# Moving a prologue's adaptive vectors from VectorE to single-column matmuls on TensorE

## The chip, the cores and the metric

The kernel runs on one core of a Trainium2 chip. A core has TensorE (PE, matmuls, with PEld for its weight loads), VectorE (DVE), ScalarE (ACT), GpSimd (POOL) and SyncE (SP), which here issues the weight transfers. The metric is the device time of one execution in microseconds (us). Three runs of the kernel before took 2280.79, 2285.01 and 2287.35 us, median 2285.01.

## The reference

Two transformer-like blocks run one after the other over the same activations x (256 tokens, 1024 features), two layers each, in float32. This case touches only the first half of each layer of the first block:

```
ada = silu(c) @ w_ada[l] + b_ada[l]                 # c: one vector of 1024; w_ada: 1024 x 6144
sh_m, sc_m, g_m, sh_f, sc_f, g_f = split(ada, 6)    # six vectors of 1024
h = rms_norm(x, norm_mix[l]) * (1 + sc_m) + sh_m
q_a, kc_a, vc_a, ks_a, ..., q_b, k_b, v_b, g_br = split(h @ w_in[l])
y_a = nsa_mixer(...)     # compressed keys and values: gelu(blocks @ w1) @ w2; selected; window
y_b = moba_mixer(...)
```

The first norm needs sh_m and sc_m of layer 0, that is the first 2048 of the 6144 columns of `silu(c) @ w_ada[0]`. Nothing of the projections can start before it.

## The kernel before

Each engine has its own program in one file, written out by hand, and they meet only at semaphores (`sig` and `at`). Nothing is scheduled by a planner.

**Panels.** All weights stream through `ring`, three slots of 1 MB (128 partitions x 2048 floats), in the order of the list that `weight_panels` makes. SyncE waits until the panel three places earlier is `released` and issues the next. A "split" panel is cut in a high and a low part for exact float32 products: ScalarE copies the high part to `parts` (L647), VectorE subtracts to get the low part (L2009, "parts<-ring,parts"), which also releases the slot. `parts` has two slots, so ScalarE first waits until TensorE has used the panel two places earlier. TensorE then does three products per weight and chunk (L1329). "raw" panels (the first weights of the compression, `cw1`) are read from the ring by TensorE itself (L1560), and TensorE's last matmul on one releases it.

**Prologue.** The adaptive columns come in groups of 512, each in two panels of 4 x 128 rows. In layer 0 the groups 0 to 3 lead the list. VectorE multiplies every 128 x 512 piece by one element per partition of silu(c) and adds it up in `sq` (L2013, L2018), and TensorE sums the 128 partitions by four matmuls with a column of ones (`ada_cols`, L1340). A float32 matmul of this kind is two passes, hence x8 in the profile. After all four groups the norm starts: one chunk of 128 features after the other is scaled and shifted on VectorE, its high part goes through ScalarE, its low part back through VectorE. The rotation angles (`angles`, then Sin on ScalarE) come after the norm.

**Projections.** `first_block` runs the column groups of w_in in the order 1, 0, 2, 3 (`ORDER`): group 1 holds the compression's inputs; `blocks` on VectorE lays them out after four transposes per kind ("tr blk"), eight additions "feat<-psum,pe_t". The eight steps of group 2 are interleaved with the 32 matmuls of the compression's hidden layer (`hidden_steps`), keys and values both. ScalarE applies gelu to them, then Sigmoid to the gates, then goes on to group 3's panels. TensorE turns q and the selected keys while group 3 runs.

**Attention.** A loop over 24 heads follows (`head_steps`, LAG 2): per turn TensorE makes one head's scores, turns the probabilities of the head two earlier, weights the values of the one before that, and takes two steps of later projections (`beside`, 12 matmuls of 512 columns per turn at first, PSUM banks 2 and 3). The compressed branch is threaded through at given turns. PSUM banks are taken by `open_bank`, which waits until the last holder of the bank is freed.

The steps of the prediction touch the first projections in both layers (0 and 1) of the first block, since `first_block(l)` runs for both, and the prologue, which is there once.

## Time and profile before

| | |
|---|---|
| median of three runs | 2285.01 us |
| the profiled execution | 2285.55 us, of which the span of its instructions 2283.7 us |
| PE / PEld busy | 2086.5 us (91%) / 1965.8 us (86%) |
| DVE / ACT / POOL busy | 1471.2 us (64%) / 993.5 us (44%) / 27.5 us (1%) |
| DMA | 372.84 MB, mean 163 GB/s |
| mean granted TensorE clock | 0.945 of full |

"Busy" is an average over stages with different limits. The prologue is a small part of the span and is limited by other things than the rest.
### The profile page before, as it was taken

How to read it: one execution, taken by the hardware profiler on the slowest of the kernel's cores; microseconds unless marked ns; L12 is line 12 of the kernel's file. 1: busy time of each engine (PE TensorE's matmuls, PEld its weight loads, DVE VectorE, ACT ScalarE, POOL GpSimd, SP SyncE). 2: the span in 40 equal slices, each digit the busy share in tenths (PEclk: the TensorE clock that was granted, in tenths of full speed). 3: DMA queues.
4: the chain of work that ended last, by engine and by line, in shares of the span. 5: the costliest groups of instructions: out<-in, count | busy, mean ns of one | idle time of the engine just before them, and what ended most of it. 6: DMA issues, size and time to landing. Idle time of an engine off the chain costs nothing. (4 is left out here: it accounts for less than half of the span.)

```text
span 2283.7 us, 36579 instructions
## 1 busy us (share of the span) xinstructions
PE 2086.5 (91%) x15232; PEld 1965.8 (86%) x15232; DVE 1471.2 (64%) x2521; ACT 993.5 (44%) x1502; POOL 27.5 (1%) x47
## 2 busy tenths in 40 slices
PE   3799979997799889999999988899999997788999
PEld 2668879997679879999998777799999996678999
DVE  6568667876577566547756576577567657555773
ACT  2355534333445433334335554543343445554342
POOL 0101000000001000000000000000000000000000
PEclk7899999999889999999999998999999998799999
DMA  8335547883544347555555323355555553232554
GB/s 285 127 133 197 182 129 247 260 278 121 167 147 168 122 137 228 181 183 183 182 175 190 119 74 111 111 167 185 179 174 183 175 163 107 74 102 83 185 180 134
DMA packets 266086, 372.84 MB, mean 163 GB/s; under 512 B 8385, under 2 KB 160193, under 8 KB 265921
## 3 DMA queue, kind: packets, MB, share of 16 engines
q1 hardware_dynamic: 264224, 367.48, 49.3%
q8 instruction: 121, 1.98, 0.4%
q10 hardware_dynamic: 1696, 3.02, 0.4%
q14 instruction: 45, 0.36, 0.0%
HBM read 369.41 MB, written 1.05 MB: 162 GB/s over the span
## 5 line engine op out<-in xcount | busy, mean ns | idle before, releaser
L2009 DVE TENSOR_TENSOR parts<-ring,parts 128x2048 fp32r<-128x2048 f32 (+4 forms) x307 | 677.7, 2209 | 471.1 <-ACT parts L647 470.7
L1329 PE MATMUL psum<-h,parts 128*128 128x256 f32 x7656 | 937.7, 284 | 27.2 <-DVE parts L2009 20.8
L1329 PEld LDWEIGHTS psum<-h,parts 128*128 128x128 f32 x7656 | 926.9, 193 | 30.2 <-issue 29.7
L647 ACT ACTIVATE parts<-ring 128x2048 fp32r<-128x2048 f32 (+3 forms) x308 | 569.5, 1849 | 863.6 <-PE psum L1329 781.7
L1329 PE MATMUL psum<-hid_hl,parts 128*128 128x256 f32 x3168 | 378.9, 282 | 1.1 <-DVE parts L2009 1.1
L1329 PEld LDWEIGHTS psum<-hid_hl,parts 128*128 128x128 f32 x3168 | 377.0, 188 | 2.0 <-issue 1.9
L1329 PE MATMUL psum<-parts,h 128*128 128x512 f32 (+1 forms) x960 | 256.3, 426 | 49.1 <-DVE parts L2009 49.1
L1329 PEld LDWEIGHTS psum<-parts,h 128*128 128x128 f32 x960 | 196.3, 214 | 93.7 <-issue 28.6
L2228 DVE CUSTOM_DVE_ANT_0 scores_area<-psum,const 128x128 f32<-128x128 f32 (+1 forms) x144 | 45.5, 353 | 102.6 <-PE psum L1497 102.6
L1497 PE MATMUL psum<-feat 64*128 64x128 f32 (+4 forms) x320 | 81.1, 380 | 15.4 <-ACT feat L647 10.0
L647 ACT ACTIVATE scores_area<-scores_area,nmax 128x256 f32<-128x256 f32 (+1 forms) x160 | 72.0, 453 | 45.9 <-DVE nmax L2228 45.4
L2009 DVE TENSOR_TENSOR rot<-psum,rstd 128x256 f32<-128x256 f32 x176 | 66.5, 419 | 38.7 <-PE psum L1329 33.4
L647 ACT ACTIVATE scores_area<-psum 128x384 f32<-128x384 f32 (+1 forms) x80 | 39.6, 498 | 107.5 <-PE psum L1509 107.4
L1497 PEld LDWEIGHTS psum<-feat 64*128 64x128 f32 (+2 forms) x320 | 48.1, 205 | 30.2 <-ACT feat L647 11.9
L2009 DVE TENSOR_TENSOR hid_hl<-rot,hid_hl 128x256 fp32r<-128x256 f32 x132 | 56.1, 425 | 4.5
L1329 PE MATMUL psum<-y_ab,parts 128*128 128x256 f32 x384 | 51.1, 298 | 7.4 <-DVE parts L2009 3.6
L1329 PE MATMUL psum<-y_mix,parts 128*128 128x256 f32 x384 | 51.5, 296 | 6.6 <-DVE y_mix L2009 3.4
L1329 PEld LDWEIGHTS psum<-y_ab,parts 128*128 128x128 f32 x384 | 50.2, 205 | 8.2 <-DVE parts L2009 3.8
L1522 PE MATMUL psum<-tok,scores_area 128*128 128x64 f32 (+1 forms) x368 | 51.3, 279 | 6.1 <-ACT scores_area L647 4.2
L1329 PEld LDWEIGHTS psum<-y_mix,parts 128*128 128x128 f32 x384 | 49.5, 201 | 7.2 <-DVE y_mix L2009 3.8
L2018 DVE SCALAR_TENSOR_TENSOR feat<-ring,scol,feat 128x512 f32<-128x512 f32 x70 | 53.3, 762 | 3.2
L2018 DVE SCALAR_TENSOR_TENSOR tok<-ring,scol,tok 128x512 f32<-128x512 f32 x70 | 52.6, 752 | 3.2
(224 smaller groups left out, 1669.1 us busy)
## 6 DMA issues: line engine op xcount, KB each, us to landing
ring<-in_w_ada SPq DMA_DIRECT2D x48, 1024.0 KB, 5.4
ring<-in_w_ffn_in SPq DMA_DIRECT2D x88, 512.0 KB, 5.0
ring<-in_ffn_w_gate SPq DMA_DIRECT2D x88, 512.0 KB, 4.0
ring<-in_ffn_w_up SPq DMA_DIRECT2D x88, 512.0 KB, 5.0
ring<-in_w_in SPq DMA_DIRECT2D x36, 1024.0 KB, 5.1
ring<-in_ffn_w_down SPq DMA_DIRECT2D x32, 1024.0 KB, 5.0
ring<-in_w_ffn_out SPq DMA_DIRECT2D x16, 1024.0 KB, 5.0
ring<-in_ffn_w_down SPq DMA_DIRECT2D x16, 768.0 KB, 4.4
```

Of the source, the lines that this page charges most:

```text
L647: act.activation(out, in_, func, **kw).then_inc(*sig(name, *keys))
L1329: mm = pe.matmul(out, left, right, start=start and n == 0, stop=stop and n == 2, skip_group_check=True)
L1497: mm = pe.matmul(b[:, a:c], head["q"][:, P * t:P * t + P], head["k"][:, 0:c - a], start=True, stop=True)
L1522: mm = pe.matmul(head["o"][t], prob_t[:, (base + i) % 2, o:o + P], head["v"][n], start=n == 0, stop=o == c - P)
L2009: dve.tensor_tensor(out, a, b, op).then_inc(*sig(name, *keys))
L2018: dve.scalar_tensor_tensor(out=out, in0=a, scalar=s, in1=b, op0=op0, op1=op1, **kw).then_inc(*sig(name, *keys))
L2228: dve.tensor_tensor_reduce(to, of, add, -scale, 3.0e38, ALU.add, ALU.min, nmax[:, n % 3, t:t + 1]).then_inc(*sig("dve_nmax", *keys))
```

## The change

- The panels of the adaptive groups come in the order 2, 3, 0, 1 (the scale vector first, then the shift), the last group behind the panels of w_in's group 1.
- VectorE's products go. TensorE reads the raw panels from the ring: 16 matmuls per panel (4 row chunks x 4 column blocks), weights 128 x 128 from the panel, one moving column of silu(c) (`first_ada`). Its last matmul releases the panel. The matmuls of the norm's statistics stand behind the first group, group 1 behind three of the eight steps of w_in's first group. The norm takes its vectors in two portions (`vectors`).
- `angles` and the Sin run ahead of everything.
- Of the constants the first 416 columns are loaded at the start; the other 1416, the rows of gains (864 KB), `pe_t` and `w2` are issued by SyncE after the eleventh panel.
- The raw panels of the compression are spread through the panel list. Its hidden layer is split: keys beside group 2, values beside group 3. Gelu and the gates' Sigmoid on ScalarE stand behind group 3's evacuation. The compressed branch comes some turns later in the attention loop. VectorE splits both panels of group 0 before the heads and blocks of group 1.

```diff
-ADA_FIRST = 4
+ADA_FIRST = (2, 3, 0, 1)
...
-CONSTS = (("ident", 128), ("ones", 128), ("tri", 128), ("causal", 384), ("chunked", 384),
...
+CONSTS = (("ident", 128), ("ones", 128), ("tri", 128), ("inv", 32), ("causal", 384),
...
+N_FIRST = 416
...
+    for i in ADA_FIRST:
+        for n in range(2):
+            src = rows(w["w_ada"][0])[:, 4 * n:4 * n + 4, 512 * i:512 * i + 512]
+            out.append((("ada", 0, i, n), "first", [(0, src)]))
+    late = out[6:]
+    del out[6:]
     for l in range(L):
         win = w["w_in"][l]
         for i in ORDER:
             group(("win", l), i, win, EDGES[i], EDGES[i + 1])
...
+            out += late
+            late = []
+            if i >= 2:
+
+                kv, name = i - 2, ("nsa_cmp_k_w1", "nsa_cmp_v_w1")[i - 2]
+                for n in range(2):
+                    src = rows(w[name][l])[:, CMP // 2 * n:CMP // 2 * n + CMP // 2, :]
+                    out.insert(len(out) - 1 + n, ((("cw1", l), kv, n), "raw", [(0, src)]))
...
+                if n == 10:
+
+                    for name, dst, src in (
+                            ("masks", const[:, N_FIRST:N_CONST], w["const"][:, N_FIRST:N_CONST]),
+                            ("rows", rowsb[:], w["rows"].broadcast_to([P, N_ROW])),
+                            ("pe", pe_t[:], w["pe_t"]), ("w2", w2[:], w["w2"])):
+                        sp.dma_start(dst, src).then_inc(
...
+            def first_ada(i):
+
+                key = ("ada", 0, i)
+                b = open_bank(key, (BANKS + i,))
+                for half in range(2):
+                    v = raw((*key, half), 4, 512)
+                    pe.wait_ge(*at(("panel", (*key, half))))
+                    for c in range(4):
+                        for j in range(4):
+                            mm = pe.matmul(b[:, j:j + 1], v[:, c, P * j:P * j + P],
+                                           scol[:, 4 * half + c:4 * half + c + 1],
+                                           start=half + c + j == 0, stop=half == 1 and c == 3,
+                                           skip_group_check=True)
...
                 if l == 0:
+                    pe.wait_ge(*at("silu c"))
+                    first_ada(ADA_FIRST[0])
                     stats(st, squares, 4)
                     stats(st, squares, DC, 4, psum[:, tally.banks[("stats", st)], :])
-                    for i in range(ADA_FIRST):
-                        ada_cols(0, i, (BANKS + i,))
+                    for i in ADA_FIRST[1:3]:
+                        first_ada(i)
...
-                whole_of(win(1))
+                steps = win(1)
+                if l == 0:
+                    advance(steps, 3)
+                    first_ada(ADA_FIRST[3])
+                whole_of(steps)
...
                 for i in ORDER:
-                    splits.until((("win", l), i, 1), 1 if i == 1 else 2)
+                    splits.until((("win", l), i, 1), 2)
```

How the instructions stand on TensorE at the start of the program, before: eight matmuls with the squares of x, then four groups of four, each waiting for VectorE's sum, then the projections.

```order
L1317 MATMUL psum<-tok,const 128x256 [waits act_squares,dve_step,load_const]
L1317 MATMUL psum<-tok,const 128x256 [waits act_squares] x7
L1340 MATMUL psum<-const,sq 128x1 [waits dve_ada]
L1340 MATMUL psum<-const,sq 128x1 x3
L1340 MATMUL psum<-const,sq 128x1 [waits dve_ada]
L1340 MATMUL psum<-const,sq 128x1 x3
L1340 MATMUL psum<-const,sq 128x1 [waits dve_ada]
```

And now ("scol" is silu(c), "panel0" to "panel2" are the landings of the ring's slots):

```order
L1584 MATMUL psum<-scol,ring 128x1 [waits act_step,panel0,dve_step,load_const]
L1584 MATMUL psum<-scol,ring 128x1 x15
L1584 MATMUL psum<-scol,ring 128x1 [waits panel1]
L1584 MATMUL psum<-scol,ring 128x1 x15
L1323 MATMUL psum<-tok,const 128x256 [waits act_squares] x8
L1584 MATMUL psum<-scol,ring 128x1 [waits panel2]
L1584 MATMUL psum<-scol,ring 128x1 x15
L1584 MATMUL psum<-scol,ring 128x1 [waits panel0]
L1584 MATMUL psum<-scol,ring 128x1 x15
```

Six panels of 16 matmuls stand ahead of the first projection, two more after its third step; before, there were 16 matmuls of this kind in all.

On ScalarE, at the end of group 3 of layer 0, before ("feat<-psum" of 15 columns is the gelu, "gates" the Sigmoid, "parts<-ring" the high part of a panel, "rs" the reciprocal roots of the heads of group 3):

```order
L647 ACTIVATE feat<-psum 128x2x15 [waits pe_hidden]
L647 ACTIVATE feat<-psum 128x4x15 [waits dve_step,pe_hidden]
L647 ACTIVATE feat<-psum 128x4x15
L647 ACT_TABLE_LOAD
L647 ACTIVATE gates<-tok 128x48 [waits act_tok]
L914 ACT_TABLE_LOAD
L647 ACTIVATE parts<-ring 128x2048 [waits pe_tokens,panel2]
L647 ACTIVATE feat<-psum 128x512 [waits pe_turned] x2
L647 ACTIVATE feat<-psum 128x256 [waits pe_turned]
L647 ACTIVATE tok<-psum 128x512 [waits pe_tokens]
```

And now:

```order
L651 ACTIVATE sq<-psum 128x512 [waits dve_ss]
L651 ACTIVATE parts<-ring 128x2048 [waits pe_tokens,panel0]
L651 ACTIVATE rs<-ss 128x8 [waits dve_ss]
L651 ACTIVATE rs<-rs 128x8 [waits act_step]
L651 ACTIVATE rs<-ss 128x8 [waits dve_ss]
L651 ACTIVATE rs<-rs 128x8 [waits act_step]
L651 ACT_TABLE_LOAD [waits dve_step]
L651 ACTIVATE feat<-psum 128x2x15 [waits pe_hidden]
L651 ACTIVATE feat<-psum 128x4x15 [waits dve_step,pe_hidden]
L651 ACTIVATE feat<-psum 128x4x15
```

The gelu now stands behind the last high part and the roots of group 3. On TensorE the attention of layer 0 now begins so ("act_hidden" is the gelu, the 12 matmuls of 512 columns are `beside`):

```order
L1503 MATMUL psum<-feat 128x128 [waits act_sq,act_copied]
L1503 MATMUL psum<-feat 128x256
L1335 MATMUL psum<-parts,h 128x512 [waits dve_lo,act_sq,act_hidden]
L1335 MATMUL psum<-parts,h 128x512 x11
L1480 MATMUL psum<-const,tok 128x128 [waits dve_head,act_sq]
```

The wait for "act_hidden" is there before too, but there the gelu stands ahead of group 3. In layer 1 the first scores themselves wait for it.

## Rows read from the trace of the kernel before

**Rows 1.** Windows view, start; columns: stretch, length, busy time per engine, PEclk, DMA share, GB/s.

```profile
14.00:41.00 27.00, 12.08 (x48) 10.46 (x48) 23.26 (x37) 5.11 (x11) 0.00 (x0) 0.69 1.01 353
```

**Rows 2.** Timeline, prologue; columns: start us, busy us, engine, line, operation, count, idle before.

```profile
13.84 5.58 PE L1317 MATMUL psum<-tok,const 128*128 128x256 f32 x16 [13.84 <-ACT tok L647]
14.55 0.49 DVE L2013 TENSOR_SCALAR sq<-ring,scol 128x512 f32<-128x512 f32 x1 [13.42 <-DMA ring<-in_w_ada]
...
20.67 1.05 PE L1340 MATMUL psum<-const,sq 128*128 128x1 f32 x8 [1.24 <-DVE sq L2018]
...
38.73 1.86 PE L1340 MATMUL psum<-const,sq 128*128 128x1 f32 x8 [4.18 <-DVE sq L2018]
...
42.84 1.00 DVE L2018 SCALAR_TENSOR_TENSOR rot<-x,gcol,rstd 128x256 f32<-128x256 f32 x2
...
47.05 4.49 DVE L2009 TENSOR_TENSOR parts<-ring,parts 128x2048 fp32r<-128x2048 f32 x2
...
49.39 13.89 PE L1329 MATMUL psum<-parts,h 128*128 128x512 f32 x48 [8.79 <-DVE parts L2009]
```

**Rows 3.** DMA issues of 0 to 120 us: KB each, median us from issue to landing.

```profile
ring<-in_w_in SPq DMA_DIRECT2D x8, 1024.0 KB, 5.1
...
const<-in_const ACTq DMA_DIRECT2D x1, 916.0 KB, 6.2
rowsb<-in_rows ACTq DMA_DIRECT2D x1, 864.0 KB, 8.3
```

**Rows 4.** Windows view of line L1329 alone: the same matmuls at both clock levels.

```profile
50.00:55.00 5.00, 5.00 (x13) 3.94 (x12) 0.50 0.94 316
56.00:62.00 6.00, 6.00 (x29) 4.95 (x28) 1.00 0.01 3
```

**Rows 5.** Windows view, all engines: 32 matmul passes of 16 columns, and what follows.

```profile
140.60:143.90 3.30, 3.18 (x33) 3.18 (x33) 3.23 (x4) 0.07 (x1) 0.00 (x0) 1.00 0.13 14
144.00:150.70 6.70, 6.70 (x22) 5.35 (x22) 2.75 (x11) 1.36 (x5) 0.00 (x0) 0.50 0.83 305
```

**Rows 6.** Timeline, layer 0 from 63 us on: TensorE and VectorE.

```profile
63.82 2.29 DVE L2009 TENSOR_TENSOR parts<-ring,parts 128x2048 fp32r<-128x2048 f32 x1 [3.66 <-ACT parts L647]
...
75.35 4.90 DVE L2009 TENSOR_TENSOR feat<-psum,pe_t 64x256 f32<-64x256 f32 x8 [4.48 <-PE psum L1474]
80.28 3.53 DVE L2009 TENSOR_TENSOR parts<-ring,parts 128x2048 fp32r<-128x2048 f32 x2
...
82.63 8.04 PE L1329 MATMUL psum<-parts,h 128*128 128x512 f32 x30 [6.95 <-DVE parts L2009]
...
90.51 0.97 PE L1560 MATMUL psum<-feat,ring 128*128 128x30 f32 x8
...
108.98 7.71 PE L1329 MATMUL psum<-parts,h 128*128 128x512 f32 x24 [5.66 <-DVE parts L2009]
```

**Rows 7.** Timeline of TensorE, layer 1.

```profile
576.53 8.53 PE L1329 MATMUL psum<-parts,h 128*128 128x512 f32 x30 [7.92 <-DVE parts L2009]
...
602.06 8.58 PE L1329 MATMUL psum<-parts,h 128*128 128x512 f32 x24 [3.46 <-DVE parts L2009]
...
617.67 0.40 PE L1618 MATMUL psum<-w,feat 128*16 128x64 f32 x4
...
628.42 0.20 PE L1474 MATMUL psum<-const,kcn 16*128 16x16 f32 x1 [2.15 <-DVE kcn L2009]
```

**Rows 8.** Timeline, layer 0, around the start of its attention.

```profile
112.51 1.28 ACT L647 ACT_TABLE_LOAD   x1
...
124.00 0.40 PE L1618 MATMUL psum<-w,feat 128*16 128x64 f32 x4
...
125.54 3.02 PE L1329 MATMUL psum<-parts,h 128*128 128x512 f32 x12
...
131.08 0.21 ACT L647 ACTIVATE rs<-rs 128x8 f32<-128x8 f32 x1
```

**Rows 9.** The page's costliest groups: ScalarE's high halves.

```profile
L647 ACT ACTIVATE parts<-ring 128x2048 fp32r<-128x2048 f32 (+3 forms) x308 | 569.5, 1849 | 863.6 <-PE psum L1329 781.7
```

More of the change, by code:

```diff
@@ L161, in wide @@
             group(name, g, a, c, min(c + width, a.shape[1]), deep)
-    def ada(l, i):
-        for n in range(2):
-            out.append((("ada", l, i, n), "ada",
-                        [(0, rows(w["w_ada"][l])[:, 4 * n:4 * n + 4, 512 * i:512 * i + 512])]))
     def between(first, stage, every):
@@ L684, in normed_hi @@
             def normed_hi(st, chunks, dst):
-                for c in range(chunks):
+                for c in chunks:
                     act.wait_ge(*at(("piece", st, c)))
@@ L697, in norm @@
                       (lambda: splits.until((first, g, 0))) if prior else None)
[L698 to L699 removed]
+                if prior:
+                    splits.until((first, g, 1))
+                    normed_hi(st, range(DC), h)
+                else:
+                    splits.until((first, g, 0))
+                    normed_hi(st, range(4), h)
+                    splits.until((first, g, 1))
+                    normed_hi(st, range(4, DC), h)
             n_sq = [0]
@@ L874, in _ @@
             run(scol[:], c8, ACT.Silu, "act_step", "silu c")
+            act.wait_ge(*at("angles"))
+            run(trig[:], turn[:, 0:2], ACT.Sin, "act_trig", "trig")
             act.preload_act_table_set(EXP_LN)
@@ new lines, in first_ada @@
+            def first_ada(i):
+                key = ("ada", 0, i)
+                b = open_bank(key, (BANKS + i,))
+                for half in range(2):
+                    v = raw((*key, half), 4, 512)
[6 more added lines that the diff above has]
+                                           skip_group_check=True)
+                    mm.then_inc(*sig("pe_ada", ("released", (*key, half)),
+                                     *([("full", key)] if half else [])))
@@ L2072, in ada_add, with norm @@
                         stt(acc, v[:, k, :], c, acc, ALU.mult, ALU.add, "dve_ada", *keys)
-            splits = Splits(split, ada_add, 2 * ADA_FIRST)
-            def norm(st, chunks, gain, dst, src, shift=None, first=None, g=0):
+            splits = Splits(split, ada_add)
+            def norm(st, chunks, gain, dst, src, shift=None, first=None, g=0, vectors=None):
                 dve.wait_ge(*at(("ln", st)))
@@ L2085, in norm, with low @@
                 refine(rstd[:], newton[:, 0, :], newton[:, 1, :])
+                if vectors is not None:
+                    vectors(0)
                 late = 1 if shift else 0
+                def low(i):
+                    keys = [("h", st, i)] + [("h", st, "last")] * (i == chunks - 1)
+                    dve.wait_ge(*at(("h hi", st, i)))
+                    tt(dst[:, 1, i, :], piece[:, i % 4, :], dst[:, 0, i, :].bitcast(F32),
+                       ALU.subtract, "dve_normed", *keys)
                 for c in range(chunks + 2 + late):
@@ L2090, in norm @@
                         settle()
+                    if vectors is not None and c == 5:
+                        low(2)
+                        low(3)
+                        vectors(1)
                     if c < chunks:
@@ L2093, in norm @@
                             ALU.mult, *([] if shift else ["dve_piece", ("piece", st, c)]))
+                    if vectors is not None and c == 2:
+                        splits.until((first, g, 0))
                     if shift and 1 <= c <= chunks:
@@ L2097, in norm @@
                     i = c - 2 - late
-                    if 0 <= i < chunks:
-                        keys = [("h", st, i)] + [("h", st, "last")] * (i == chunks - 1)
-                        dve.wait_ge(*at(("h hi", st, i)))
-                        tt(dst[:, 1, i, :], piece[:, i % 4, :], dst[:, 0, i, :].bitcast(F32),
-                           ALU.subtract, "dve_normed", *keys)
+                    if 0 <= i < chunks and not (vectors is not None and i in (2, 3)):
+                        low(i)
                     if i == 1 and first is not None:
@@ L2490, in first_block @@
                            ("free", ("vc", l)))
-                    if i in (1, 7):
-                        heads_in(3, i // 7, ks_mq[i // 7])
-                    if i == 3:
+                    if i == 4:
+                        ks_mk = [head_sums(8, HD) for t in range(TT)]
+                    if i:
+                        for _ in range(UNITS):
+                            next(more, None)
+                    if i in (1, 3):
+                        heads_in(3, i // 3, ks_mq[i // 3])
+                    if i == 5:
                         for g in range(2):
```

204 lines of the change are left out of this document (85 added, 119 removed).

## The prediction

> **What bounds the kernel now.** I read the windows view of the start first, then the timeline there, then the timeline of both layers' projections, and last the DMA issues. In the prologue VectorE and the transfers run abreast: from 14 to 41 us VectorE is busy 23.3 of 27 us and the DMA share is 1.01 [rows 1]. TensorE has little to do. Then a chain sets the pace: last sum of an adaptive group at 38.73 + 1.86 = 40.6, norm from there, first chunk at 42.84, VectorE's low parts of two panels in 4.49 us at 47.05, first projection at 49.39, its 48 matmuls over at 63.3 [rows 2]. After it TensorE sets the pace with holes, for each of which VectorE's low part came last: 6.95 us before 82.63, 5.66 before 108.98, and in layer 1 7.92 before 576.53 and 3.46 before 602.06 [rows 6, 7]. Those holes and the start of the attention are where the change acts a second and third time.
>
> **Part 1: the adaptive vectors on TensorE.** The first panel is in use on VectorE at 14.55 [rows 2]. Ahead of it now go 1416 of 1832 columns of constants less (708 of 916 KB), 864 KB of rows and 144 KB of the two small loads, 1.76 MB; at the 353 GB/s of that stretch [rows 1] to about 390 that is 4.5 to 5 us, so TensorE starts at 10.1.
> The price of a matmul with one column: the burst of four (eight passes) took 1.05 us at 20.67 and 1.86 us at 38.73, as the two between them [rows 2]; less the tail of the last pass (a quarter and a third of a us) that is 0.114 us a pass at full clock and 0.215 at half clock. A panel is 16 matmuls, 32 passes: 3.65 or 6.9 us. VectorE was busy 23.3 us with the eight panels and little else [rows 1], some 2.9 a panel. So the question is the clock.
> Between 140.72 and 144 TensorE did 32 passes of 16 columns, busy 3.18 of 3.30 us at clock 1.00, and right after it the clock is 0.50 for the whole 6.7 us, with TensorE busy throughout [rows 5]. A panel of single columns is the same 32 passes with fewer columns. The bursts of single columns before 38.73 did not lift it either [rows 2]. I take half clock: 6.9 us.
> The Trainium skill, "TensorE: Matmul & The Clock Gate", Part 1, section "What's actually happening", says that the clock follows how busy the engine has been and that sustained activity releases the throttle; by that a TensorE kept busy for 40 us by such matmuls runs at full clock, and the sum below would lose 24 us. The row above stands against that reading here. The same page's section on LDWEIGHTS gives 128 / 1.2 = 107 ns for a load of 128 columns with no word of the clock; by that a pass would cost 0.107 us even when cold, while the bursts show 0.215.
> The chain is then: start 10.1; two panels 13.8; the statistics' 16 passes 5.9 (5.58 in the row, where the rate doubles on the way [rows 2]; the bounds are all at full or all at half clock, 3.5 to 6.8): 29.8. Four panels 27.6, less 3 because the 256-column passes lift the clock for a while, as they did before: 54.4. Then the norm: take and first chunk 0.3, three chunks and the first low part at 3.2 + 2.3 us as in the rows from 42.84 on: first projection at 60.1. Three steps of six matmuls: the 512-column matmul costs 5.00 / 12 = 0.42 us at half and 6.00 / 27 = 0.225 at full clock [rows 4] (the counts take in those cut by the edges); mostly cold, 6.5: 66.6. Two panels of group 1 with some 3 us at full clock after the steps: 10.9 instead of 13.8: 77.5. Chunks 4 to 7 of the norm come 3.1 us after that, the fourth step hides most of it; five steps end 9.9 later at 87.4. Before, this point is 63.3: **+24.1 us**. Bounds: +20 and +30 (all stretches cold). The transfers stay ahead of this, since a panel lands 5.1 us after its issue [rows 3] and waits 6.9 for its turn; that cover also hides the moved 1.7 MB. Angles and Sin now lie in the wait for the first panels; they cost nothing.
>
> **Part 2: projections, layer 0.** Group 0's panels are split before the blocks, so the hole of 6.95 us goes. What is late next is group 2's low part: second panel of group 0 low at 91.8, heads of group 1 4.6 (from 63.82 + 2.29 to where the idleness before 75.35 begins), blocks 4.9, low part 1.3 (3.53 less 2.29 for the two at 80.28) [rows 6]: 102.6, against 99.4 when TensorE is ready: hole 3.3. Group 2 with half of the hidden matmuls is 8 steps of 0.77 + 0.45 us (four passes, half of the 0.97 in [rows 6]): 112.5. Group 3's first panel needs the slot that the keys' raw half frees at 107.6: + 5.1 landing [rows 3] + 1.9 high [rows 9] + 2.3 low = 117.0, a hole of 4.5 (before 5.66). Group 3 with the other hidden half and the transposes is 15.9. In it the turn of the selected keys waits for a copy that stands on ScalarE behind the high part of a panel whose slot frees only half a group earlier: 5.1 + 1.9 + 0.5 against 4.7 us of work, a hole of 2.9. After each hole some ten matmuls run cold, 0.195 us each [rows 4]: 3.9 for two. Sum: 139.7 against 124.00 [rows 8]: **+15.7** in place of +24.1, so this part gives back 8.4 (bounds 4 to 13).
>
> **Part 3: start of the attention, both layers.** The gelu followed a table load that was over at 113.8 [rows 8], and the wait for it was free. Now it stands behind group 3's roots, which end at 131.08 + 0.21 = 7.3 us after group 3's end, plus table load 1.28 [rows 8] and 0.3: 8.9 us. In that time TensorE can do the first scores only; before, the 12 matmuls started 1.5 us after group 3 [rows 8]. The next scores and with them VectorE's masks queue behind it. Against that the wait for the compressed keys (2.15 us before 628.42 in layer 1 [rows 7], the like in layer 0) goes. The third scores start 20.2 us after group 3 instead of 11, as the 12 matmuls run cold after 8 us of idleness: +9.2 in layer 0. In layer 1 the first scores wait too: 21.5 instead of 10.9, less 3 for some fifteen matmuls that ran cold behind the keys' wait before: +7.6. Bounds for each: 0 (if something else held it anyway) and +12.
>
> **Part 4: projections, layer 1.** By the same steps the hole of 7.92 us becomes 2.1 and the ten cold matmuls after it go (2.0), the 3.46 becomes 4.4, the wait for the copy adds 2.9, and 1 comes from a short wait for a raw panel: group 3 ends at 612.7 against 617.67 [rows 7]: **-5.0**.
>
> **Part 5: the rest of the loop.** VectorE and ScalarE catch up in the new waits and later turns find them less behind: -2 a layer, -4 (0 to -8).
>
> **Sum:** 15.7 + 9.2 - 5.0 + 7.6 - 4 = +23.5 on the profiled execution's 2285.55 us, which is 0.5 above the median: **2309 us**.
>
> **Rivals.**
> A. Full clock through the single-column matmuls. Each panel 3.65 us; the clock still needs its first rise: group 0 ends at 38, first projection 43.6, end of the first group 63.5 instead of 87.4. 2309 - 24 = 2285, no change. For it speaks the page's rule above; against it [rows 5] and the cold bursts.
> B. The gelu's wait is hidden, because VectorE's masks or the next panel hold TensorE there anyway: 2309 - 16.8 = 2292. For it: VectorE was behind at this place before, the roots, which the masks follow, came 7.3 us after group 3. Against: the queue of part 3 is in the program's order.
> C. The other side: a pass costs less than even the full-clock burst of rows 2 shows, since a long row of loads pipelines better than eight. Then the transfers pace the prologue at 2.9 us a panel, group 0 is done at 27, the first projection starts at 33 and its group ends at 48, 39 us ahead of my chain: 2270 to 2272. It decides for faster from about 3.5 us a panel on; rows show 3.65 at best.
> D. The change spoils more than counted: every bound on the slow side, 2325 to 2335.
>
> **Chances.** Forecast (2297 to 2321) 0.63, A 0.12, B 0.13, C 0.05, D and others 0.07. The range of 2283 to 2324 leaves out C, part of A, and D. A measurement of this kernel tells about 0.3% (7 us) from no change. Slower: the forecast, D and half of B, 0.75. Same: most of A and half of B, 0.14. Faster: C and the low end of A and of the unknown in part 5, 0.11.
>
> **What would show it.** Right: single-column passes about 0.21 us apart at clock 0.50 for most of 10 to 54 us, first projection near 60, its group over near 87; the hole before the second half of group 0 gone in both layers; TensorE idle about 8 us after the first scores of either layer, ended by the gelu. Wrong: passes 0.11 apart (A), closer still (C), `beside` starting 1 to 3 us after group 3 (B). What breaks the forecast first is the clock in the prologue.

## The result and the profile after

The changed kernel takes 2311.74 us (median of 4, 2309.25 to 2321.58) against 2283.82 of before: ratio 1.0119, interval 1.0100 to 1.0138. It is slower, by 28 us or 1.2%; the forecast was 2309. The profiled execution took 2309.25 us, the lowest of the four, its span 2307.4, mean granted clock 0.947: its rows account for 23.7 us of the 28. Below, "cold" means at a granted clock of 0.50 and "warm" at 1.00.

The timeline of TensorE in the changed kernel, start (L1584 are the single-column passes, L1323 the statistics, L1335 the projections; columns as in [rows 2]):

```profile
10.00 13.78 PE L1584 MATMUL psum<-scol,ring 128*128 128x1 f32 x64 [10.00 <-DVE turn L2049]
23.65 5.64 PE L1323 MATMUL psum<-tok,const 128*128 128x256 f32 x16
29.12 22.48 PE L1584 MATMUL psum<-scol,ring 128*128 128x1 f32 x128
57.43 4.97 PE L1335 MATMUL psum<-parts,h 128*128 128x512 f32 x12 [5.83 <-DVE h L2043]
...
64.67 10.11 PE L1584 MATMUL psum<-scol,ring 128*128 128x1 f32 x64
...
78.17 13.03 PE L1335 MATMUL psum<-parts,h 128*128 128x512 f32 x48 [0.62 <-DVE h L2043]
```

The first group's 64 passes take 0.215 us each. The first projection starts at 57.43, before at 49.39 [rows 2]. The x48 of the last row are the second half of group 1 and the first of group 0. Until the clock rises at 82.20 (next view) some 9.5 of them run at the 0.42 us of [rows 4], the other 14.5 of group 1 at 5.71 / 24 = 0.24: it ends near 85.7, where before it was 63.3.

The windows view of the same stretch, by the clock (columns as in [rows 1]; the first row's 1.00 lies ahead of the first record of a change and says nothing):

```profile
10.00:27.58 17.58, 17.58 (x73) 16.82 (x74) 0.64 (x3) 4.20 (x10) 0.00 (x0) 1.00 0.60 205
27.58:34.41 6.83, 6.83 (x57) 6.62 (x55) 1.86 (x5) 0.80 (x2) 0.00 (x0) 1.00 0.16 45
34.41:61.72 27.31, 21.48 (x92) 20.57 (x92) 8.21 (x16) 5.38 (x6) 0.00 (x0) 0.50 0.56 190
...
68.54:82.20 13.66, 13.04 (x46) 11.09 (x47) 6.15 (x13) 3.47 (x5) 5.92 (x15) 0.50 0.56 199
```

The clock is at 1.00 from 27.58, during the 256-column passes of the statistics. Of the 57 passes in the second row 49 are single-column ones, in the 5.29 us from 29.12 on: 0.108 us each. At 34.41 the clock falls, although TensorE is not idle, and it stays at 0.50 while TensorE is busy without a break until 51.6.

The further timeline, both layers, the rows with a wait (they answer to [rows 6 to 8]):

```profile
100.48 1.01 PE L1335 MATMUL psum<-parts,h 128*128 128x280 f32 x6 [2.94 <-DVE parts L2043]
...
115.00 2.90 PE L1335 MATMUL psum<-parts,h 128*128 128x512 f32 x6 [4.58 <-DVE parts L2043]
...
132.28 0.44 PE L1480 MATMUL psum<-const,tok 128*128 128x128 f32 x2 [3.09 <-ACT feat L651]
...
137.81 0.92 PE L1503 MATMUL psum<-feat 64*128 64x128 f32 x4
146.18 5.00 PE L1335 MATMUL psum<-parts,h 128*128 128x512 f32 x12 [7.45 <-ACT feat L651]
...
167.19 1.36 PE L1503 MATMUL psum<-feat 64*128 64x128 f32 x4 [2.34 <-DVE nmax L2273]
...
572.71 18.68 PE L1335 MATMUL psum<-parts,h 128*128 128x512 f32 x72 [9.00 <-DVE parts L2043]
...
600.67 1.45 PE L1335 MATMUL psum<-parts,h 128*128 128x280 f32 x6 [2.93 <-DVE parts L2043]
...
617.73 2.90 PE L1335 MATMUL psum<-parts,h 128*128 128x512 f32 x6 [5.54 <-DVE parts L2043]
...
634.44 0.44 PE L1480 MATMUL psum<-const,tok 128*128 128x128 f32 x2 [2.96 <-ACT feat L651]
...
648.53 1.62 PE L1503 MATMUL psum<-feat 64*128 64x128 f32 x4 [8.47 <-ACT feat L651]
```

The holes of 6.95 us in layer 0 and 7.92 in layer 1 are gone; in layer 0 waits of 2.94, 4.58, 3.09 and 7.45 us stand now, in layer 1 of 2.93, 5.54, 2.96 and 8.47.

To place a difference, the table gives for each kernel how much later than before (us) the same work starts in its one profiled execution: first and last scores of layer 0's attention, first and seventeenth of layer 1's, and the end of the span.

| kernel | ratio to before (interval) | L0 first | L0 last | L1 first | L1 17th | end |
|---|---|---|---|---|---|---|
| changed | 1.0119 (1.0100-1.0138) | 13.1 | 22.0 | 30.2 | 30.1 | 23.7 |
| e1 vectors only | 1.0047 (1.0035-1.0060) | 15.4 | 18.3 | 20.5 | 17.6 | 13.2 |
| e2 loop only | 1.0033 (1.0021-1.0045) | 5.6 | 6.4 | 13.3 | 8.5 | 4.2 |
| e3 clock filler | 1.0163 (1.0144-1.0182) | 30.1 | 39.1 | 47.8 | 47.3 | 40.7 |
| e4 gelu first | 1.0098 (1.0084-1.0112) | 19.0 | 24.3 | 23.4 | 26.0 | 25.4 |
| e7 gelu behind high part | 1.0091 (1.0069-1.0112) | 13.8 | 18.4 | 22.2 | 20.1 | 19.5 |
| e9 panel moving | 1.0070 (1.0047-1.0093) | 1.6 | 10.6 | 18.2 | 16.2 | 15.6 |
| e12 hidden back | 1.0050 (1.0032-1.0067) | 17.8 | 15.7 | 17.1 | 14.3 | 7.7 |
| e5 low parts ahead | 0.9941 (0.9921-0.9961) | -10.1 | -14.8 | -14.9 | -17.9 | -18.0 |
| e10 and late turns | 0.9946 (0.9927-0.9964) | -10.0 | -9.5 | -8.0 | -10.8 | -10.8 |
| e6 vectors on VectorE | 0.9932 (0.9909-0.9955) | -10.0 | -7.1 | -6.1 | -9.1 | -12.4 |
| e11 all of these | 0.9927 (0.9907-0.9948) | -10.0 | -11.9 | -10.2 | -13.0 | -19.7 |
| e13 and filled hole | 0.9869 (0.9851-0.9886) | -17.2 | -16.8 | -22.5 | -25.3 | -28.5 |

Executions of one kernel mostly differ by 8 to 18 us (before: 2281.65 to 2290.51 in one set of 15; e5: 2264.34 to 2282.08 in 9), and a profiled execution lies up to 6 us from its kernel's median (e2 and e12 6 below, e6 5 above). So a column of the table is good to some 5 us, and the ratios decide.

### The profile page after: what moved, and what is told of

Its sections match the earlier page's. It is cut to its first block and busy times, and to the rows that moved or that the text cites. A ratio compares the mean times of both kernels' runs of the same rounds, so it can differ in the third digit from the quotient of the medians.

```text
span 2307.4 us, 36992 instructions
## 1 busy us (share of the span) xinstructions
PE 2121.8 (92%) x15456; PEld 2003.3 (87%) x15456; DVE 1450.0 (63%) x2489; ACT 990.2 (43%) x1500; POOL 24.2 (1%) x47
## 3 DMA queue, kind: packets, MB, share of 16 engines
HBM read 369.41 MB, written 1.05 MB: 161 GB/s over the span
## 5 line engine op out<-in xcount | busy, mean ns | idle before, releaser
L1335 PE MATMUL psum<-h,parts 128*128 128x256 f32 x7656 | 939.0, 285 | 27.3 <-DVE parts L2043 20.9
L1335 PEld LDWEIGHTS psum<-h,parts 128*128 128x128 f32 x7656 | 928.2, 193 | 30.2 <-issue 29.7
L1335 PE MATMUL psum<-hid_hl,parts 128*128 128x256 f32 x3168 | 379.1, 282 | 1.1 <-DVE parts L2043 1.1
L1335 PEld LDWEIGHTS psum<-hid_hl,parts 128*128 128x128 f32 x3168 | 377.0, 188 | 2.2 <-issue 1.9
L1335 PE MATMUL psum<-parts,h 128*128 128x512 f32 (+1 forms) x960 | 259.6, 427 | 43.7 <-DVE parts L2043 28.9
L1335 PEld LDWEIGHTS psum<-parts,h 128*128 128x128 f32 x960 | 194.4, 213 | 87.6 <-issue 40.0
L1503 PEld LDWEIGHTS psum<-feat 64*128 64x128 f32 (+2 forms) x320 | 48.0, 204 | 43.1 <-issue 15.7
L1335 PE MATMUL psum<-y_mix,parts 128*128 128x256 f32 x384 | 51.5, 295 | 6.6 <-DVE y_mix L2043 3.4
L1335 PE MATMUL psum<-y_ab,parts 128*128 128x256 f32 x384 | 49.5, 292 | 7.5 <-DVE parts L2043 3.6
L1335 PEld LDWEIGHTS psum<-y_ab,parts 128*128 128x128 f32 x384 | 48.6, 199 | 8.2 <-DVE parts L2043 3.8
L1335 PEld LDWEIGHTS psum<-y_mix,parts 128*128 128x128 f32 x384 | 49.5, 201 | 7.2 <-DVE y_mix L2043 3.8
L1584 PE MATMUL psum<-scol,ring 128*128 128x1 f32 x256 | 46.4, 318 | 10.0 <-DVE turn L2049 10.0
L1584 PEld LDWEIGHTS psum<-scol,ring 128*128 128x128 f32 x256 | 46.5, 287 | 10.1 <-issue 10.0
```

The costliest lines, as they stand in the source:

```text
L1335: mm = pe.matmul(out, left, right, start=start and n == 0, stop=stop and n == 2, skip_group_check=True)
L1503: mm = pe.matmul(b[:, a:c], head["q"][:, P * t:P * t + P], head["k"][:, 0:c - a], start=True, stop=True)
L1584: mm = pe.matmul(b[:, j:j + 1], v[:, c, P * j:P * j + P], scol[:, 4 * half + c:4 * half + c + 1], start=half + c + j == 0, stop=half == 1 ...
```

## The experiments

**e1_vectors_only.** The prologue's part of the change, as in the diff ahead; hidden products, gelu, raw panels, turns and VectorE's run-ahead as before.

```diff
+            out += late
+            late = []
             if i == 2:
                 tail = out.pop()
```

> Only the prologue's part of the change (vectors on TensorE from raw panels, split constants, angles early, norm with its vectors in two parts); projections and attention in the order of before. Theory (the single-column passes at half clock cost what the change costs): group 1's projections end about 21 us later than 63.3, the holes of layer 0 before 82.6 and 109 stay as they were, so the attention starts about +21 and the whole takes +18 to +22: 2302 to 2306. Rival (the later parts of the change cause most of it, the prologue's delay is absorbed in layer 0's holes, since VectorE is free earlier): +8 or less, under 2293.

2298.86 us, 12.5 above the runs beside it. The prologue is as in the full change (first projection at 57.72), and the attention starts 15.4 later. The 21 us at the end of group 1 became 15 by the end of group 0's first half, because before had there a wait of 2.98 us and cold matmuls behind it. TensorE's timeline, before:

```profile
66.25 8.55 PE L1329 MATMUL psum<-parts,h 128*128 128x512 f32 x24 [2.98 <-DVE parts L2009]
```

and e1 (the same 24 are the second half of these 48):

```profile
78.85 11.15 PE L1337 MATMUL psum<-parts,h 128*128 128x512 f32 x48 [0.53 <-DVE h L2040]
```

The result lies between the two, and both theories had a part of it: the delay arises in the prologue, and a third is absorbed. Between layer 1's first scores and the end it stands 7 us less behind; I have no row that says why.

**e2_loop_only.** The other part: everything behind the prologue, with the vectors on VectorE.

```diff
+            if i >= 2:
+                kv, name = i - 2, ("nsa_cmp_k_w1", "nsa_cmp_v_w1")[i - 2]
...
-                steps, hidden = win(2), hidden_steps(l)
+                steps, hidden = win(2), hidden_steps(l, 0)
...
-                steps = win(3)
+                steps, hidden = win(3), hidden_steps(l, 1)
```

> Only the loop's part: raw panels spread, hidden products a half in groups 2 and 3, gelu and gates behind group 3, kc and the turns later, group 0's low parts ahead of the blocks; vectors on VectorE as before. Theory: layer 0's projections end about 8 us earlier (the hole of 6.95 us goes), its attention's first turns give 9 back (gelu wait), layer 1's projections end 1 to 5 us earlier and its attention gives 8 back; whole time -6 to +6 of before: 2278 to 2290. Rival 1 (the gelu wait is hidden anyway): -14 or more, 2270 or less. Rival 2 (the loop's part is what costs): +12 or more, 2296 or more.

2295.91 us, 9.5 above before: the loop's part alone costs, more than I had worked out. The two parts together make 0.80% against 1.19% for the full change; the other 0.39%, some 9 us (3 to 15 by the intervals), belongs to neither part alone, and no run here explains it.

**e5_low_parts_ahead.** One line of the loop's part alone.

```diff
-                    splits.until((("win", l), i, 1), 1 if i == 1 else 2)
+                    splits.until((("win", l), i, 1), 2)
```

> The kernel before with one edit: VectorE makes the low parts of both panels of group 0 ahead of the blocks (run-ahead 2 in place of 1). Theory: the hole of 6.95 us before group 0's second half goes as it did with the loop's part alone (group 2 starts some 8 us earlier in layer 0), and, since the hidden products and the gelu stay where they were, nothing of it is paid back at the start of the attention: -6 in layer 0, -4 in layer 1, whole 2276 (2272 to 2280). Rival (what is late next, group 3's first panel, takes it back): within 2 us of before.

2271.56 us, 15.8 below the runs beside it (13.5 by the ratio), up to half as much again as I expected. Beside e2 it shows where that kernel loses. TensorE, group 3 and the attention's start, e5:

```profile
98.89 7.17 PE L1329 MATMUL psum<-parts,h 128*128 128x512 f32 x24 [5.76 <-DVE parts L2009]
...
109.45 0.44 PE L1474 MATMUL psum<-const,tok 128*128 128x128 f32 x2 [1.15 <-ACT feat L647]
...
113.91 0.40 PE L1618 MATMUL psum<-w,feat 128*16 128x64 f32 x4
...
114.61 0.92 PE L1497 MATMUL psum<-feat 64*128 64x128 f32 x4
115.45 3.02 PE L1329 MATMUL psum<-parts,h 128*128 128x512 f32 x12
```

and e2:

```profile
98.77 2.90 PE L1327 MATMUL psum<-parts,h 128*128 128x512 f32 x6 [6.10 <-DVE parts L2013]
...
116.23 0.44 PE L1472 MATMUL psum<-const,tok 128*128 128x128 f32 x2 [3.22 <-ACT feat L644]
...
130.26 1.62 PE L1495 MATMUL psum<-feat 64*128 64x128 f32 x4 [8.43 <-ACT feat L644]
```

Group 3 starts at 98.8 in both, since its first panel comes when it comes; the time that half of the hidden products left in group 2 went into a longer wait before group 3, 6.10 us for 5.76. Then group 3 takes 15.0 us in e5 and 23.1 in e2 (half the hidden products, a wait for a copy, cold matmuls), and 8.4 us of waiting follow.

**e10_low_ahead_late_turns.** e5 with the later turns of the compressed branch, the hidden products and the gelu left where they were.

```diff
-                    if i == 1:
+                    if i == 3:
                         transposes(("tr kc", l), ...
-                    if i == 2:
+                    if i == 4:
                         pe.wait_ge(*at(("copied", ("tr kc", l))))
```

> The kernel of the low-parts run (vectors on VectorE, low parts of group 0 ahead of the blocks) with the later turn numbers of the change in the attention (kc's norm, transposes, compressed scores and weights, mq), while hidden products, kc and vc products, gelu and raw panels stay where they were. Theory (what made the loop's part slow are the hidden half and the gelu behind group 3, not the turns): the third scores of layer 0 start 1 to 2 us earlier than with the low parts alone, since the wait of 2.15 us for the compressed keys goes; whole 2270 (2264 to 2276). Rival (the late turns cost, by the wait for the masks before the fifth scores that the changed kernel shows, 2.3 us, or later): 4 us or more above the low parts alone, 2276 or more.

2274.47 us, ratio 0.9946 against 0.9941 of e5: the turns neither help nor hurt measurably (in the profiled execution the wait of 2.15 us goes, and the third scores start 2.3 us earlier than in e5, but a wait of 3.81 us for VectorE's masks follows, and the sixth start 3.5 later). So what e2 has and e10 has not, the hidden half and the gelu behind group 3 with the raw panels spread, costs 0.87%, 20 us over the two layers.

**e12_hidden_back.** The full change with just that put back.

```diff
-                steps, hidden = win(3), hidden_steps(l, 1)
+                steps = win(3)
```

> The changed kernel with the hidden products, kc and vc products, the gelu with the gates and the raw panels put back where the kernel before has them (both halves in group 2, gelu ahead of group 3's copies); vectors on TensorE, low parts ahead and late turns stay. Theory (the hidden half and the gelu behind group 3 cost some 20 us over both layers, as the loop's part alone stands against the run with low parts and late turns: 1.0033 against 0.9946): whole near 2287, first scores of layer 0 at 131 to 135 in place of 137.8, no wait of 7.45 us behind them. Rival (in the full change that cost is mostly hidden, since the late prologue has shifted the transfers): 2300 or more.

2299.32 us (2288.93 to 2300.88): 16 below the changed kernel by the ratios, not 25. The waits for the gelu are gone, but the first scores start at 142.5, not at 131 to 135, since group 2 ran cold from end to end (below, e6 and e13). Neither theory alone holds: the cost is there, and part of what its removal gives is lost to the clock.

**e4_gelu_first and e7_gelu_behind_high_part.** The changed kernel with ScalarE's gelu, gates and table load moved, in e4 ahead of group 3's copies, in e7 behind them and the next high part, ahead of the roots.

```diff
-                squared = win_out(3)
-                splits.until((("win", l), 3, 1), 2)
-                rsqrts(squared)
-
                 for kv in range(2):
                     job = ("hid", l, kv)
...
                 act.preload_act_table_set(EXP_LN)
+
+                squared = win_out(3)
+                splits.until((("win", l), 3, 1), 2)
+                rsqrts(squared)
```

That is e4; in e7 only the line with `rsqrts` moves.

> The changed kernel with ScalarE's gelu, gates and the table load behind them ahead of group 3's copies and roots, not behind. Theory (the wait for the gelu sets the start of the attention): the hole of 7.45 us before the 12 matmuls of layer 0 and that of 8.47 in layer 1 shrink to under 4 us; the roots come some 4 us later, so that about half is given back: whole 2302 to 2307. Rival (something else held TensorE there, the heads and masks of VectorE): the hole stays or its name changes, whole within 2 us of 2311 or above it.

> The changed kernel with ScalarE's gelu, gates and table load ahead of group 3's roots alone, behind its copies and the next panel's high part. Theory (TensorE waits there for the bank that the hidden half holds until the gelu has read it; the copies of group 3 must not wait for it): the wait after the first scores ends 4 us earlier than in the changed kernel, the roots come 1 to 2 us later; layer 0's and layer 1's attention start 3 to 4 us earlier: whole 2304 (2300 to 2308). Rival (the masks of VectorE, behind the roots, set the pace): no gain, 2310 to 2313.

e4: 2310.94 us, e7: 2305.89. TensorE's timeline behind layer 0's first scores, e4:

```profile
149.11 4.43 PE L1335 MATMUL psum<-parts,h 128*128 128x512 f32 x12 [4.55 <-issue]
```

e7:

```profile
142.93 4.61 PE L1335 MATMUL psum<-parts,h 128*128 128x512 f32 x12 [3.56 <-ACT feat L651]
```

and ScalarE's timeline in e4:

```profile
144.10 1.28 ACT L651 ACT_TABLE_LOAD   x1
145.40 0.24 ACT L651 ACTIVATE gates<-tok 128x48 f32<-128x48 f32 x1
145.66 1.28 ACT L923 ACT_TABLE_LOAD   x1
146.95 0.60 ACT L651 ACTIVATE tok<-psum 128x512 f32<-128x512 f32 x1
...
148.40 0.62 ACT L651 ACTIVATE sq<-psum 128x512 f32<-128x512 f32 x1
```

The next matmuls need two PSUM banks. One is held by the hidden layer until its gelu has read it: the gelu of the keys ends at 142.87 in e7 and at 146.13 in the changed kernel, and TensorE starts some 0.05 us after it. The other is held by group 3's second tokens until their square is done. In e4 the profile names no releaser, but that square ends at 149.02 and TensorE starts at 149.11, 5 us after the last gelu. So in the changed kernel and in e7 the gelu comes last, in e7 3.3 us earlier, and in e4 the copies: from the first to the last scores of layer 0 the changed kernel loses 8.9 us to before, e4 5.3, e7 4.6. In e4 the whole did not follow: its first scores came 5.9 us later than the changed kernel's, before the edit has any effect (four panels took 24.84 us in place of 22.48, and group 2 started cold), and its median, 2310.94, lies above the forecast 2302 to 2307. e7's median lies in its range of 2300 to 2308. By the ratios e4 stands 5 us and e7 6 us below the changed kernel, and both intervals overlap the changed kernel's at the edge. The wait is a real term, worth 4 us in e7's rows of layer 0; the whole agrees with it but does not prove it.

**e3_clock_filler and e9_panel_moving.** Two tests of the clock. In e3, behind every four single-column matmuls, four idle ones of 256 columns:

```diff
                                            skip_group_check=True)
+                        if i != ADA_FIRST[3]:
+                            warm(4, psum[:, 3, 256:512])
```

> The changed kernel with four idle bf16 matmuls of 256 columns after every four single-column ones in groups 2, 3 and 0 (96 of them, into an unused bank). Theory (the passes are slow because the clock is at half): the filler lifts the clock to 1.00 for most of 10 to 50 us, a single-column pass falls to 0.114 us, a panel takes 3.65 + 16 x 0.107 = 5.4 us in place of 6.9; first projection about 9 us earlier, whole 2302. Rival 1 (the clock does not rise with it): 6.9 + 3.4 = 10.3 us a panel, +20: 2331. Rival 2 (clock 1.00, but a pass takes 0.21 us at any clock): 8.6 a panel, +10: 2321.

In e9 the panel moves through and the silu column stands still:

```diff
-                            mm = pe.matmul(b[:, j:j + 1], v[:, c, P * j:P * j + P],
-                                           scol[:, 4 * half + c:4 * half + c + 1],
+                        mm = pe.matmul(row, scol[:, k:k + 1], v[:, c, :], start=k == 0,
+                                       stop=k == 7)
```

> The changed kernel with the operands of the vector products swapped: the silu column is the stationary operand (128 x 1), the panel's 512 columns move through, 8 matmuls of 512 columns a group in place of 64 passes of one column; the row that comes out is copied by VectorE and turned into columns by four small matmuls. Theory (the prologue is slow because single columns leave the clock at half): the clock rises to 1.00 within the first group and stays, a panel takes 3.4 us in place of 6.9 (6.8 if it stayed at half), group 1 ends some 20 us earlier, whole 2291 (2286 to 2298). Rival (the clock stays at half in the prologue whatever TensorE does there): 2310 to 2318. Second rival (the transfers cannot feed it): panels 5 us apart, 2300 or so.

e3 took 2326.62 us, e9 2301.51. The timeline of e3, the same instructions at both levels:

```profile
28.37 1.01 PE L1315 MATMUL psum<-idle 128*128 128x256 bf16 x4
...
35.20 0.95 PE L1584 MATMUL psum<-scol,ring 128*128 128x1 f32 x8
36.01 0.60 PE L1315 MATMUL psum<-idle 128*128 128x256 bf16 x4
...
58.25 1.71 PE L1584 MATMUL psum<-scol,ring 128*128 128x1 f32 x8
```

and of e9:

```profile
10.45 9.83 PE L1583 MATMUL psum<-ring,scol 128*1 128x512 f32 x16 [10.45 <-DVE turn L2062]
20.21 3.72 PE L1323 MATMUL psum<-tok,const 128*128 128x256 f32 x16
23.86 7.03 PE L1583 MATMUL psum<-ring,scol 128*1 128x512 f32 x16
...
46.52 4.74 PE L1335 MATMUL psum<-parts,h 128*128 128x512 f32 x12 [5.83 <-DVE h L2056]
```

with the windows view of its second group:

```profile
24.00:31.00 7.00, 7.00 (x18) 1.36 (x16) 2.45 (x6) 0.77 (x2) 0.00 (x0) 1.00 0.43 140
```

In e3 the eight passes take 0.95 us behind the statistics and 1.71 at half clock, the four fillers 0.60 and 1.01: what a pass costs goes with the clock alone, and the second rival falls. But the filler did not hold the clock: it fell between 41 and 42, with TensorE busy throughout, and the kernel paid for the fillers, nearly as its first rival said (2331). In e9 the same bytes are worked through by matmuls of 512 columns; the clock rises within the first group and stays up until the norm, a panel takes 3.5 us, and the first projection starts at 46.5 in place of 57.4. Group 1 ends near 74.0 in place of 85.7, 11.7 us of the 20 I expected, and the time lies above the range of 2286 to 2298: the first group still took 9.83 us, and the row's copy and the turn into columns cost 3.0 (1.05 and 1.94 for the small matmuls) with a wait of 3.58 behind group 1.

**e6_vectors_on_vectore and e11_best.** The vectors back on VectorE, with the parts of the prologue's change that do not depend on them: constants in two loads, late loads, early angles; and e5's line. e11 has e10's turns too.

```diff
+            angles()
             dve.wait_ge(*at("silu c"))
             for i in range(ADA_FIRST):
...
-            for name, dst, src in (("const", const[:], w["const"]),
+            for name, dst, src in (("const", const[:, 0:N_FIRST], w["const"][:, 0:N_FIRST]),
```

> The kernel before with the constants in two loads, the rows, masks and small loads moved behind SP's eleventh panel, angles and Sin in the wait for the first panel, and the low parts of group 0 ahead of the blocks; the first adaptive vectors stay on VectorE, the loop in the order of before. Theory: VectorE starts its first panel near 10.1 in place of 14.55 and keeps its pace of 2.9 us a panel, first projection near 45 in place of 49.4: another -4 on e5: 2272 (2267 to 2277). Rival (the panels then land later than VectorE wants them, since they share the transfers): no more than e5 alone.

> The same with the constants in two loads, the moved loads and the early angles as in the run with the vectors on VectorE. Theory: the prologue's 3.7 us come on top of the low parts and the turns: 2267 (2260 to 2274), the fastest of all. Rival (the earlier start of the projections is lost in group 3's late first panel): as the run before it, within 2 us.

2268.41 and 2269.26 us: no faster than e5 by their intervals. The first projection does start 3.7 us earlier (45.70), but the gain is not passed on. Windows view of group 2 in layer 0, e6:

```profile
73.40:98.20 24.80, 24.80 (x112) 24.80 (x113) 11.17 (x22) 6.77 (x11) 0.00 (x0) 0.50 0.47 151
```

and e5:

```profile
79.40:93.10 13.70, 13.70 (x112) 13.41 (x112) 8.63 (x21) 3.92 (x9) 0.00 (x0) 1.00 0.70 223
```

The same 112 matmuls, TensorE busy in every microsecond of both, at half clock from end to end in the one and at full in the other. In e11 and e12 the stretch is cold as well, in both layers, behind a wait of 2.9 us. In e5 and e10 it is warm in layer 0, behind a wait of 1.1, but cold in layer 1, where the wait before it is 2.89. TensorE's timeline of e5, start and end of group 2 in layer 1:

```profile
562.25 1.33 PE L1329 MATMUL psum<-parts,h 128*128 128x280 f32 x6 [2.89 <-DVE parts L2009]
...
586.68 7.30 PE L1329 MATMUL psum<-parts,h 128*128 128x512 f32 x24
```

That is 24.4 us, where layer 0 took 13.7. The first six matmuls still ran partly warm (1.33 us; 1.75 is cold, 1.02 warm), so there the clock fell inside the group.

**e13_filled_hole.** e11 with that wait filled.

```diff
+                    b = open_bank(("hid", l, kv))
+                    if kv == 0:
+                        warm(24, b[:, 256:512])
+                        yield
```

> The fastest kernel so far (vectors on VectorE, constants split, low parts ahead, late turns) with 24 idle bf16 matmuls of 256 columns in the 2.9 us in which TensorE waits before group 2, in each layer. Theory (in the profiled runs at 2265.9, 2273.2 and 2293.2 us the whole of group 2 ran at clock 0.50 for 24.8 us, though busy throughout, and in others at 1.00 for 13: the idleness before it decides): with the filler group 2 of layer 0 runs at 1.00 and takes 13 us; group 3's wait for its first panel, 5.7 us, comes back, so the first scores start about 5 us earlier, near 110; whole 2264 (2260 to 2268). Rival (the clock falls at this place whatever runs in the hole): group 2 at 0.50 still, first scores at 115 or later, whole 2269 to 2272.

2257.04 us (2253.54 to 2259.80), 30 below the kernel before: faster than before and than e11, by 13 us against e11 (by the ratios), and below the range of 2260 to 2268. Timeline of e13:

```profile
70.67 2.79 PE L1313 MATMUL psum<-idle 128*128 128x256 bf16 x24
73.76 1.00 PE L1333 MATMUL psum<-parts,h 128*128 128x280 f32 x6 [0.30 <-DVE parts L2018]
...
91.76 7.20 PE L1333 MATMUL psum<-parts,h 128*128 128x512 f32 x24 [4.34 <-DVE parts L2018]
```

and its windows view of group 2:

```profile
73.00:86.50 13.50, 13.20 (x111) 12.83 (x108) 8.39 (x19) 3.92 (x9) 0.00 (x0) 1.00 0.62 198
```

Group 2 takes 13.5 us in place of 24.8, group 3 waits 4.3 us for its panel again, and the first scores come 7.1 us earlier than in e11, in layer 1 12.3.

The rows of all kernels together say more than this pair. A step of group 2 is six passes of 280 columns with the hidden layer's passes behind them. Where both halves of the hidden layer stand in the group (eight passes of 30 columns a step) and TensorE has just waited 2.88 to 2.90 us, the group was cold from its first or second step to its end in eight of eight cases: both layers of e6, e11 and e12, layer 1 of e5 and e10. Behind a wait of at most 1.13 us it was warm in four of four: layer 0 of e5 and e10, both layers of e13. Where only the keys' half stands there (four a step), a wait of 2.92 to 2.94 us was followed in eleven cases by a warm group twice (layer 0 of the changed kernel and of e9), by a start that was cold or soon fell and turned warm again within two to four steps seven times, and by a cold group to the end twice (e3). TensorE's timeline of e4, layer 0, one of the seven:

```profile
103.79 1.19 PE L1335 MATMUL psum<-parts,h 128*128 128x280 f32 x6 [2.94 <-DVE parts L2043]
...
107.75 1.75 PE L1335 MATMUL psum<-parts,h 128*128 128x280 f32 x6
...
111.78 1.01 PE L1335 MATMUL psum<-parts,h 128*128 128x280 f32 x6
```

## Why the prediction was right

The time is within 3 us of the forecast. The mechanism of parts 1 to 3 is in the rows; part 4 failed, and part 5 was a guess without a row. That the sum fits so closely is partly luck: part 4 came out 3.7 us above its term and parts 1 and 5 together 2.4 below theirs. By the medians the change cost 28 us, 4 more than forecast.

- *Part 1, the vectors on TensorE, +24.1 at the end of group 1.* Start 10.0 (10.1), first group 13.78 us (13.8), statistics 5.64 (5.9), four panels 22.48 (24.6), first projection 57.43 (60.1), end near 85.7 (87.4): +22.4. A cold pass costs 0.215 us, and the clock stays at half for most of the prologue, as [rows 5] had it. Rival A falls by the changed kernel's own rows: 64 passes in 13.78 us, and clock 0.50 from 34.41 on. Rival C falls by the same rows and by the cost of a pass at full clock, 0.108 us there and 0.95 / 8 = 0.12 in e3. Against the Trainium skill ("TensorE: Matmul & The Clock Gate", Part 1, "What's actually happening": activity releases the throttle, so sustained work should bring full clock) stand the passes from 34.41 to 51.60, and 73.40:98.20 of e6 more plainly: busy throughout, clock 0.50.
- *Part 2, layer 0's projections, holes of 3.3, 4.5 and 2.9 us.* Measured 2.94, 4.58 and 3.09; first scores at 137.81 against 139.7. From the end of group 1 that is 52.1 us for 52.3, so the part itself is right almost to the number. Against before the first scores come 13.1 us later, for +15.7 in the sum: 1.7 of the difference is part 1's, and 0.7 comes from taking 124.00 of before, where a product stands that the change has moved, and not its first scores. What the sum did not show is how it is made up: e5 and e2 part it into a gain from the low parts (the group behind starts 10 us earlier) and a loss of 8 from the hidden half in group 3. I had netted the two.
- *Part 3, the wait for the gelu, +9.2 and +7.6.* Measured 7.45 and 8.47 us of waiting, and from first to last scores of layer 0 +8.9; in layer 1, up to the seventeenth, about +7.7 (30.1 less 23.7 at the layer's entry, and less the -1.3 of part 4). Right in size. The steps were not quite as forecast: the third scores of layer 0 start 18.0 us after group 3 (155.80 less 137.81), not 20.2, and some of the rest comes at the fifth, where TensorE waits 2.34 us for VectorE's masks. The prediction gave the order on ScalarE as the cause and did not say what holds TensorE there: it is the bank of the hidden keys, and the bank of group 3's second tokens stands right behind it (e4). Rival B, hidden anyway, is out: the wait is there, and e7 takes 3.3 us off its end and the layer gets 4.3 back.
- *Part 4, layer 1's projections, -5.0.* This is the term that failed: layer 1's first projection starts 23.7 us late (572.71, before 548.99), and its group 3 ends 22.4 late (640.06, before 617.67), so it gave back 1.3. The hole of 7.92 went to nothing, but 2.93 (forecast 2.1), 5.54 (4.4) and 2.96 (2.9) stand instead, 2.0 us more than forecast. And the forecast had no cold matmuls in group 2: its first two steps took 4.00 us (600.67 to 604.67), where they take 2.42 in layer 0, 1.6 us more. Together that is 3.6 of the 3.7 us.
- *Part 5, -4 for the rest.* Layer 0's last scores to layer 1's entry +1.7, layer 1's seventeenth scores to the end -6.4: -4.7 together. No row explains these; they are of the size by which executions differ, so the agreement is luck.

TensorE's timeline of before, layer 1's first projection:

```profile
548.99 18.75 PE L1329 MATMUL psum<-parts,h 128*128 128x512 f32 x72 [8.99 <-DVE parts L2009]
```

Sum: 13.1 + 8.9 + 1.7 - 1.3 + 7.7 - 6.4 = 23.7, the difference of the two spans.

What stays open: what exactly lets group 2 fall to half clock and stay there. e13 shows that filling the wait keeps it warm in that kernel. The changed kernel enters the group behind 2.94 us of waiting and is warm (six matmuls in 1.01 us at 100.48), e12 enters it behind 2.90 us and is cold. What the two have different there is the second half of the hidden layer; no run changed that alone, and e3, with one half, was cold too. Nor was the filler tried in the changed kernel, or the gelu of the keys alone moved ahead of group 3, though its input is complete there.

## What to carry to other kernels

Work moved to an engine that is idle is priced at that engine's state then, not at its best: 256 short passes on an idle TensorE cost 46 us, most of them at half clock, where VectorE had done the work abreast of the transfers. An edit bundle should be parted before it is judged: here one line (run-ahead 2 in place of 1) was worth 14 to 16 us and lay under a change that cost 28. Where a whole group of matmuls runs cold behind a short wait, two dozen idle matmuls in the wait can be worth as much as the best reordering: here 13 us.

## What the runs showed of the hardware that was not expected

- TensorE was busy in 24.80 of 24.80 us of e6's group 2 and the clock stood at 0.50 for all of it; the same instructions took 13.7 us at 1.00 in layer 0 of e5, and 24.4 in its layer 1, where the first six still ran partly warm. With both halves of the hidden layer in it the group never came back from half clock; with one half it did in seven of nine cases.
- The first group's passes with one moving column (64 in 13.78 us) ran at half speed to their end; with the panel moving and a single stationary column (e9, 16 passes of 512 columns in 9.83 us, then in 7.03) the clock came up within them.
- ScalarE's three table loads of 1.28 us each stand in the way of whatever is queued behind the gelu: they are 3.8 of the 4.6 us that the moved work takes in e7 (141.38 to 145.95).
